# Three quarters of an MLP's down product by seven products instead of eight, with its outputs summed in DRAM

## The reference, cut to what matters

```python
hdn = rmsnorm(x, p["norm_mlp"][i]) @ p["w_up"][i]                       # 1024 -> 4096
x = x + (jnp.square(jax.nn.relu(hdn)) @ p["w_down"][i]).astype(x.dtype)  # 4096 -> 1024
```

## Time and profile before

| | |
|---|---|
| time, median of 3 runs | 2321.97 us (2321.2 to 2323.86) |
| span of the profiled execution | 2320.3 us |
| PE busy / weight loads busy | 99% / 93% |
| DVE / ACT / POOL busy | 63% / 49% / 17% |
| granted PE clock | 0.998 of full speed |
| DMA | 275.28 MB, mean 119 GB/s |

### The profile page before, as it was taken

The page is one execution under the profiler, slowest core; times in us unless marked ns, Lnnn a source line. Parts: engine busy times, 40 slices in busy tenths (PEclk is TensorE's granted clock), DMA queues, the critical chain, the costliest instruction groups (busy, mean ns, idle before and its releaser), DMA issues.

```text
span 2320.3 us, 32838 instructions
## 1 busy us (share of the span) xinstructions
PE 2301.6 (99%) x12624; PEld 2154.4 (93%) x12624; DVE 1455.5 (63%) x2287; ACT 1143.6 (49%) x2248; POOL 389.5 (17%) x448
## 2 busy tenths in 40 slices
PE   8999999999999999999999999999999999999998
PEld 7999679898999999999999995998989999999997
DVE  7988784475575453636478878736756746455464
ACT  5555435555554353526446545445455544445362
POOL 1121002200112121211211110022002121212120
PEclk9999999999999999999999999999999999999999
DMA  5554327842446565655555553288215465655563
GB/s 158 115 110 108 91 86 165 183 103 63 88 112 132 127 128 123 132 127 126 119 121 109 107 124 93 69 178 180 81 46 127 101 134 117 136 127 124 122 149 101
DMA packets 111289, 275.28 MB, mean 119 GB/s; under 512 B 12630, under 2 KB 13910, under 8 KB 111140
## 3 DMA queue, kind: packets, MB, share of 16 engines
q0 software_dynamic: 63936, 116.42, 30.0%
q1 hardware_dynamic: 46628, 156.31, 22.2%
q10 hardware_dynamic: 576, 0.52, 0.1%
HBM read 270.06 MB, written 3.15 MB: 118 GB/s over the span
## 4 chain that ended last, share of the span: by engine, by line
PE 90%; DVE 6%; ACT 1%; issue 1%; DMA 1%; SPq 0%; DVEq 0%; ACTq 0%
PE G L1216 44%; PE G L1770 3%; PE M L1731 3%; PE M L1737 3%; PE G L1731 3%; PE G L1737 3%; PE M L1733 2%; PE G L1733 2%; PE G L1658 2%; PE M L1179 2%; PE M L1181 2%; PE M L1180 2%; PE M L1216 1%; DVE tap L1939 1%; PE M L1445 1%; PE M L1168 1%
## 5 line engine op out<-in xcount | busy, mean ns | idle before, releaser
L569 POOL DMA_DIRECT2D wlo<-wstream x332 | 292.0, 880 | 1341.0 <-ACT wlo L602 1122.8
L602 ACT ACTIVATE wlo<-raw 128x512 fp32r<-128x512 f32 x292 | 183.7, 629 | 515.2 <-PE G L1216 437.7
L1216 PE MATMUL G<-B_hi,whi 128*128 128x384 f32 x1120 | 375.6, 335 | 0.9 <-DMA wlo<-wstream 0.9
L1216 PE MATMUL G<-B_lo,whi 128*128 128x384 f32 x1120 | 374.6, 334 | 0.0
L1216 PE MATMUL G<-B_hi,wlo 128*128 128x384 f32 x1120 | 374.5, 334 | 0.0
L1216 PE MATMUL G<-A_hi,whi 128*128 128x384 f32 x864 | 294.3, 341 | 8.7 <-DVE A_lo L1899 8.2
L1216 PE MATMUL G<-A_hi,wlo 128*128 128x384 f32 x864 | 290.4, 336 | 0.0
L1216 PE MATMUL G<-A_lo,whi 128*128 128x384 f32 x864 | 285.6, 336 | 0.0
L1867 DVE TENSOR_TENSOR scaled_out<-G,rbc 128x768 f32<-128x768 f32 x56 | 53.6, 957 | 276.4 <-PE G L1216 252.0
L1216 PEld LDWEIGHTS G<-B_hi,whi 128*128 128x128 f32 x1120 | 210.3, 188 | 2.2 <-issue 2.1
L1216 PEld LDWEIGHTS G<-B_lo,whi 128*128 128x128 f32 x1120 | 210.3, 188 | 0.5 <-issue 0.5
(11 more groups left out here) (493 smaller groups left out, 4878.8 us busy)
## 6 DMA issues: line engine op xcount, KB each, us to landing
raw<-wstream SPq DMA_DIRECT2D x220, 512.0 KB, 4.1
wlo<-wstream POOLq DMA_DIRECT2D x332, 256.0 KB, 5.3
w_low<-wstream POOLq DMA_DIRECT2D x96, 256.0 KB, 4.1
raw_b<-wstream SPq DMA_DIRECT2D x32, 512.0 KB, 5.8
ring<-dft SPq DMA_DIRECT2D x8, 512.0 KB, 4.4
mraw<-memT SPq DMA_DIRECT2D x16, 256.0 KB, 3.2
X<-xT SPq DMA_DIRECT2D x8, 384.0 KB, 6.8
win<-dft SPq DMA_DIRECT2D x6, 512.0 KB, 6.3
```

What stands on the lines that cost most here:

```text
L569: pool.dma_start(low, wstream[stream(L, c)][:, part], accum_op=ALU.add).then_inc(lo_in[c % 2][h], 16)
L602: act.activation(wlo[:, s, part], raw[:, s, part], ACT.Copy, scale=-1.0).then_inc(neg_done, 1)
L1216: last = mm(out, w, p[:, k, a:b], start=(k == 0 and w is w_hi and p is parts[0]), stop=(k == KT - 1 and (w is w_lo and only is None or onl ...
```

## The change

Three quarters of the down product (3072 of 4096 hidden channels) also go by seven products. The MLP of a layer becomes 32 steps in one run, `fast_steps`: four *chunks* of three up steps and four down steps (`CHUNKS, UPS, DOWNS`), then four up steps (`LAST`) whose hidden values go to `B_hi, B_lo` as before, and one ordinary down quarter.

- An up step of a chunk doesn't write hidden values as they are, but the seven combinations that a down product needs, hi and lo, in `slices` (seven pairs for each of the three up steps, in memory of B and, for the third, of X). DVE makes four of the raw combinations, ACT seven high parts, DVE seven low parts; of these, several fall into the first products of the next step (`late`).
- A down step takes 7 products of 3 blocks x 3 matmuls of 384 columns. Its weights are 384 wide instead of 512 (`width`). It makes two output tiles of 128 x 768, which are neither scaled nor added to X: they go to a `staged` buffer, and POOL sends them to `down_sum` in DRAM (`down_out`), plainly in the first chunk and with accumulation in the other three. There are two pairs of `staged` buffers; DVE and ACT wait for the transfer from two steps before (`y_out`).
- X is written to DRAM (`x_kept`, 8 tiles) ahead of the steps, and read back after the last chunk, since its memory holds slices. The eight sums of `down_sum` are read into `y_part` at the end, and `residual` and `end_add` get one more DVE addition for each tile, with a wait for it.
- The order of the seven products is another one, for the query product of the cross-attention too: product 2 adds into the bank of product 0, three outputs are copied by ACT (`p_one`, `p_five`, `u_two`) and each of three more takes one DVE addition. The negated part of `w_low[0]` is asked for after product 2 of the step before, that of `w_low[1]` after product 3, that of `w_low[2]` after product 0 of its own step.
- `correction` is spread over down steps 4 and 5; the sum of squares on PE moves into step 3.

The core of the diff:

```diff
+CHUNKS, UPS, DOWNS, LAST = 4, 3, 4, 4
+STEP = UPS + DOWNS
+FAST = CHUNKS * STEP + LAST
+SLICE = UPS * 2 * P
@@ POOL
+                def down_out(f):
+                    r, U = down_row(f), L * FAST + f
+                    if f >= STEP and r == 0:
+                        for i in range(2):
+                            pool.wait_ge(y_out[i], 32 * outputs_before(L, f))
+                    for row in range(2):
+                        if row == 0:
+                            pool.wait_ge(u_c, 3 * U + 4)
+                        else:
+                            pool.wait_ge(u_c21, L * PAIRS + 4 + f + 1)
+                        if f < STEP:
+                            pool.dma_start(down_sum[L, 2 * r + row], staged[r % 2][row][:, :]).then_inc(y_out[r % 2], 16)
+                        else:
+                            pool.dma_start(down_sum[L, 2 * r + row], staged[r % 2][row][:, :],
+                                           accum_op=ALU.add).then_inc(y_out[r % 2], 16)
+                for f in range(FAST):
+                    pair_low(f, 0)
+                    pair_low(f, 1)
+                    if f and is_down(f - 1):
+                        down_out(f - 1)
+                    pair_low(f, 2)
@@ PE
+                        blocks_k = UPS if is_down(f) else 4
+                        newest = f == 0 or is_down(f) and down_row(f) == 0
...
+                        if f == 0:
+                            pe.wait_ge(c_hi, L * 56 + 28 + 21 + n + 1)
+                        elif newest:
+                            pe.wait_ge(u_hh, made + (1, 3, 4, 5, 6, 6, 7)[n])
...
+                        elif newest:
+                            pe.wait_ge(u_hl, made + n + 1)
+                        mm(out, high(end), src(1, end), start=False, stop=True, skip_group_check=added).then_inc(u_mm, 1)
@@ DVE, in fast_steps
+                        if is_up(f) and n == 6:
+                            dve.wait_ge(u_h, made + 4)
+                            tt(raw_[2], raw_[5], raw_[1], ALU.subtract).then_inc(u_h, 1)
+                            slice_low(f, 0, 1)
+                            tt(raw_[4], raw_[5], h_buf[2], ALU.subtract).then_inc(u_h, 1)
+                            slice_low(f, 1, 3)
+                        if f and is_up(f - 1):
+                            raw_ = slice_raw[(f - 1) % STEP]
+                            if n == 0:
...
+                                tt(raw_[6], raw_[3], raw_[2], ALU.subtract).then_inc(u_h, 1)
+                                slice_low(f - 1, 2, 4)
+                            if n == 1:
+                                slice_low(f - 1, 3, 5)
+                                slice_low(f - 1, 4, 6)
+                            if n == 2:
+                                slice_low(f - 1, 5, 2)
+                                slice_low(f - 1, 6, 7)
+                        if j < 7 * FAST - 4:
+                            weight_low(j + 4)
@@ DVE, residual
+                    dve.wait_ge(x_in[m], 16 + 32 * (scaled_in + 1))
+                    link(tt(scaled_out[:, :], out, y_part[m][:, :], ALU.add))
+                    link(tt(scaled_out[:, :], scaled_out[:, :], rbc[:, :], ALU.mult))
```

More of the change, by code:

```diff
@@ L42 @@
 XD = D // XH
-QUARTERS = 4
 EPS = 1e-5
@@ L519, in _ @@
-                query_raw(4, 0, 28 * L + 27)
+                query_raw(3, 0, LOWS * L + 20)
+                query_raw(4, 1, LOWS * L + 21)
+                query_raw(4, 0, LOWS * L + 27)
                 chunks(L, C_O, C_MLP - C_O, QUERY)
[L521 to L544, removed]
@@ new lines, in _ @@
+                sp.wait_ge(o_mm, L * 8 + 8)
+                pair(1)
+                for m in range(KT):
+                    sp.wait_ge(psum_free, L * TILES + (T_O + m + 3))
+                    sp.dma_start(x_kept[m], X[:, m, :]).then_inc(stored, 16)
+                for f in range(2, CHUNKS * STEP + 3):
+                    pair(f)
+                sp.wait_ge(stored, (L + 1) * KT * 16)
+                sp.wait_ge(u_mm, done + 7 * CHUNKS * STEP)
+                for i in range(2):
+                    sp.wait_ge(y_out[i], 32 * outputs_before(L + 1, UPS))
@@ new lines, in _, with sums @@
+                for m in range(KT):
+                    sp.dma_start(X[:, m, :], x_kept[m]).then_inc(x_in[m], 16)
+                for f in range(CHUNKS * STEP + 3, FAST + 1):
+                    pair(f)
+                def sums(first):
+                    for m in range(first, first + 4):
+                        sp.dma_start(y_part[m][:, :], down_sum[L, m]).then_inc(x_in[m], 16)
+                sp.wait_ge(u_mm, done + 7 * (FAST - 1) + 3)
+                sums(0)
+                for m in range(6 if L == DEPTH - 1 else 8):
+                    if m == 2:
+                        sp.wait_ge(u_mm, done + 7 * FAST)
+                        sums(4)
+                    c = L * CH + C_MLP + m
+                    sp.wait_ge(hi_done, c * 2 + 2)
+                    sp.dma_start(raw[:, m % 2, :], wstream[w + 2 * FAST + m + AHEAD]).then_inc(raw_in[m % 2], 16)
@@ L955, in combine @@
                     n = L * 64 + 32 + g * 8
-                    for c, ready in (((0, 1), (3, 3)), ((5, 5), (4, 6), (1, 7), (2, 4), (6, 8)))[i][first:behind]:
+                    for c, ready in (((0, 1), (3, 3)), ((4, 5), (1, 6), (5, 8), (2, 4), (6, 7)))[i][first:behind]:
                         act.wait_ge(c_src, n + ready)
@@ new lines, in slice_high, with hidden_high @@
+                def slice_high(f, i, order, ready):
+                    act.wait_ge(*ready)
+                    k = f % STEP
+                    act.activation(slices[k][0][i], slice_raw[k][i], ACT.Copy).then_inc(u_hh, 1)
+                def hidden_high(f, k, half, buf, ready):
+                    if ready is not None:
+                        act.wait_ge(u_h, hidden_count(L, f, 7, 3) + ready)
+                    act.activation(B_hi[:, 2 * (f - CHUNKS * STEP) + k, half * HALF_T:(half + 1) * HALF_T], h_buf[buf],
+                                   ACT.Copy).then_inc(u_hh, 1)
@@ new lines, in slice_low, with summed @@
+                def slice_low(f, i, ready):
+                    k = f % STEP
+                    dve.wait_ge(u_hh, hidden_count(L, f, 7, 4) + ready)
+                    tt(slices[k][1][i], slice_raw[k][i], f_(slices[k][0][i]), ALU.subtract).then_inc(u_hl, 1)
+                def summed(f, h, dst, kept, ready, bank):
+                    dve.wait_ge(ready, L * PAIRS + 4 + f + 1)
+                    tt(dst, kept, bank[:, 0:HALF_T], ALU.add).then_inc(u_c, 1)
+                    if not is_down(f):
+                        dve.wait_ge(u_c, 3 * (L * FAST + f) + h + 2)
+                        stt(out=dst, in0=dst, scalar=0.0, in1=dst, op0=ALU.max, op1=ALU.mult).then_inc(u_h, 1)
@@ new lines, in hidden_low, with correction @@
+                def hidden_low(f, k, half, buf, order):
+                    dve.wait_ge(u_hh, hidden_count(L, f, 7, 4) + order + 1)
+                    where = (slice(None), 2 * (f - CHUNKS * STEP) + k, slice(half * HALF_T, (half + 1) * HALF_T))
+                    tt(B_lo[where], h_buf[buf], f_(B_hi[where]), ALU.subtract).then_inc(u_hl, 1)
+                def correction(part):
+                    if part == 0:
+                        dve.wait_ge(st_sum, L * NORMS + 5)
+                        for (a, b), bank in zip(HALVES, (GB[3], MB[3])):
+                            link(ts(sq[:, a:b], bank[:, 0:HALF_T], 1.0 / D, EPS, ALU.mult, ALU.add))
+                    elif part < 3:
+                        link(tt(sq[:, 0:T], sq[:, 0:T], rbc[:, :], ALU.mult))
+                    else:
+                        link(dve.reciprocal(rbc[:, :], sq[:, 0:T]))
```

716 lines of the change are left out of this document (385 added, 331 removed).

## The result

The changed kernel takes 2364.57 us (median of 4 runs, 2360.21 to 2369.79) against 2322.91 for the kernel before on the same chip: ratio 1.0182, 95% interval 1.017 to 1.0195. It is **slower by 1.8%**, where 2296 us was forecast. The span of the profiled execution is 2358.4 us against 2320.3.

A forecast was written before the change was run, and what follows sets the result against it. PE was taken as the bound, busy 99%. From the 2320.3 us span, 49.9 removed and 24.1 given back (8 + 9 + 2 + 1.6 + 1 + 2.5), plus 1.7 for median over span: 2296 us, range 2274 to 2330.

The forecast's parts named there:

- PE's work: In the MLP, 288 matmuls fewer at 0.1733 us each: 49.9 us removed.
- Rival 4: PE's pace is another in products of 9, for instance by a wait at each start: 22 us, 2310; chance 0.06.
- DVE in an up step: In up steps DVE is busy 13.1 us, 90% of the step, and doesn't become the bound on average.
- Rival 2: DVE bounds the second and third up step through waiting on ACT: 2308 to 2332 us; chance 0.14.
- The seam at the first down step: From third up step to first down step PE waits for DVE's low slices: 1.0 us a chunk, 8 us.
- DMA: In down steps of chunks 1 to 3 the DMA engines are full, 93 to 107%, but keep up on average.
- The price of a sum: In down steps, accumulation into DRAM priced like accumulation into SBUF: 37 to 40 us of engine time each.
- The step that failed: In down steps w_low[0], asked for after product 2, lands at about 10.3, wanted at 10.92; waits of 9 and 2 us.
- The reciprocal: 4.95 us on DVE in a down step delays the addition product 6 needs: 0.8 us a layer, 1.6 us.
- The last parts: One more DVE operation of 256 columns lengthens the last five parts: 2.5 us (0 to 4).
- rival 3: In down steps slow accumulation into DRAM holds up low parts, kernel slower than before: 2359 to 2377 us; chance 0.13.
- The sign that I had named for it: At down steps PE's waits for w_low, 0.5 us x 18, grow to 4 us if rival 3 holds.

The follow-up runs named there:

- e9: As e8, with the 4.95 us reciprocal on DVE moved from behind product 1 of down step 5 to behind product 6 of down step 6: 2281.93 us, ratio 0.9832.
- e5: The changed kernel, still asking for w_low[0] after product 2, but raw loads of the step after next wait until product 4 is done: 2289.2 us, ratio 0.9866.
- e2: The changed kernel without the accumulating sums of chunks 1 to 3 (those outputs left out): 2363.43 us, ratio 1.0185.
- e1: The changed kernel, with w_low[0] of the next step asked for after product 0 instead of after product 2: 2310.75 us, ratio 0.9945.
- e6: The changed kernel, with w_low[0] asked for after product 0 and the sums of chunks 1 to 3 left out: 2304.92 us, ratio 0.993.
- e8: The changed kernel, with each low part asked for once its buffer is free, w_low[2] between the two sums, and raw loads after product 4: 2285.71 us, ratio 0.9845.

## Why the prediction was wrong

*PE's work.* 288 matmuls at an unchanged pace: right. e9's span is 2320.3 - 49.9 + 9.7. Rival 4 is out with it: a product of 9 that waits for nothing takes 1.56 us. (Its time was added up wrongly: 2296 + 22 is 2318, not 2310.)

*DVE in an up step.* 90% forecast, 91% in the window, no wait inside up steps. Rival 2 is out. The seam at the first down step: 1.0 us a chunk forecast for product 0 and a little for the next; from chunk 1 on it is 1.18 + 0.25 us over two layers in the changed kernel and in e5 and e9 alike, 0.7 a chunk. The reason is the one given, as the wait rows for `slice_lo` show.

*DMA.* The share of 93 to 107% in down steps: 0.94 and 0.98. The price of a sum, 37 to 40 us of engine time: in the window 905 to 955 POOL's queue has 69.1% of 800 us for 9 low parts of 192 KB, 3 of 256 KB and 8 sums; less 9 x 19.6 and 3 x 26 that leaves 37 each. Right, as far as the shares taken for the low parts hold, and nevertheless beside the point, as e2 shows.

*The step that failed* is "its own data are in at about 10.3. In time, with 0.6 to spare". I had the landing as the work in the queues divided by 16 engines, which gave 4.4 us after the asking; at the place shown it was 6.7 after the issue, and 3.8 without the raw loads in front (e5). The raw loads were in that sum only as a share of the bandwidth. What they do to a transfer issued just behind them is more than that: 2.9 us at this place, and 2.3 in the medians (6.22 against 3.95), whether the share is 0.98 or 0.54 (e2: 6.15). POOL's issue came a little late besides, 2.0 us after the start of product 2's last matmul, where I had counted 1.4 to the asking. So the term stood at 0.5 us for 18 transitions and 0.25 for 8, 11 us, and was 77.8 less the seam, some 72. Two things together made it. Asked for late without the collision, the low part is nearly always in time (e5: 7.7 us of loss, the seam in it). Asked for early, with the raw loads as they were, 24.5 us stay (e1). And as I had tied it to full engines, I gave no loss to transitions where they are half empty: in chunk 0 the step after the first up step lost 2.1 us a layer, and step 29, under the reading back of X, which I had called hidden, 4.0 a layer. Both went in e1 and e5. The rule of the Trainium skill that I weighed ("DMA: Bandwidth & Descriptors", "Queues, rings and completion order": in order within a ring, in turn between rings) is compatible with e1 against e6, where the sums ahead of `w_low[2]` cost 8.7 us at product 6. For `w_low[0]` the harm came from another queue, SP's, with which it takes turns by the same rule.

*The reciprocal.* 0.8 us a layer forecast, 1.5 found (3.1 at that product in both layers, and 3.4 to 0.3 in e9): the right mechanism, twice the size.

*The last parts.* 2.5 us forecast, some 0.5 found: from the first to the last start of the matmuls of `B_hi` with `end_hi` it is 57.0 us before (L1770) and 57.5 after (L1910). PE, not DVE, set most of that stretch.

*The sum.* 24.1 us given back were forecast; by the spans it was 2358.4 - 2270.4 = 88.0. The time fell in rival 3's range without its mechanism: a sum was no dearer than its price in SBUF, and leaving the sums out brought nothing. The sign that I had named for it, waits for `w_low` above 1.5 us with DMA at 0.9, doesn't single it out, since e2 shows the same waits at 0.54.

## What to carry to other kernels

A transfer that an engine waits for within a few microseconds isn't judged by the DMA share alone: look at what is issued close to it, on any queue, in the two microseconds ahead and, as e1 suggests without showing it alone, about one behind. Here 0.8 MB of prefetch with nearly a step of slack, sent just ahead of 192 KB with 5 us, cost 75 us in all. When an order of work is moved, look again at every DMA issue that it moves past; holding the patient one back was a one-line wait here. And when a profile shows a full resource beside the waits, leave out that load in one run before believing it.

## What the runs showed of the hardware beyond that

PE's clock. In the kernel before it was at its full level (2.4 GHz) from 100 us on until the last products. In the changed kernel it fell to half (1.2 GHz) seven times ahead of the last products, each time for a few microseconds, in six of them after stretches in which PE had been waiting. In the window at 755 us, behind two of 10 us with PE busy 8.5 and 8.0 us, it is 0.83, and 47 matmuls fit instead of 58. Such a stretch doesn't always do it: from 835 to 855 us PE was busy 8.0 and 8.0 us, and the clock of the next 10 us was 1.00.

```profile
735.00:745.00 10.00, 8.51 (x48) 7.90 (x47) 8.65 (x11) 4.38 (x10) 2.89 (x4) 1.00 0.77 211
745.00:755.00 10.00, 8.00 (x47) 7.67 (x45) 6.17 (x11) 5.76 (x11) 3.67 (x5) 1.00 0.73 180
755.00:765.00 10.00, 9.69 (x47) 9.72 (x48) 1.42 (x3) 4.08 (x8) 1.03 (x2) 0.83 0.52 143
```

The mean clock of the execution is 0.994 against 0.998; 0.4% of 2358 us is 9 us, my estimate of its part in the 91.7. In e5, e8 and e9 it is back at 0.999. I had not counted this, and it makes a wait of PE dearer than its length.
